# A two-layer diffusion backbone on one core: the first scale blocks multiplied with the weights as stationary operand, in halves

## What is computed

```python
mod_ctx = jax.nn.silu(c_ctx) @ w_mod[l] + b_mod[l]      # mod_lat likewise from c
sh1, sc1, g1, sh2, sc2, g2 = jnp.split(mod, N_MOD, axis=-1)
h = rms_norm(x, p["g_pre_mix"]) * (1.0 + sc1) + sh1
proj = h @ p["w_in"]
```

## Time and profile before

| | us |
|---|---|
| median of 3 runs | 1262.65 (1262.24 to 1262.71) |
| profiled execution | 1259.98 |
| its span, first to last instruction | 1258.2 |
| TensorE busy | 1229.9 (98%) |
| VectorE busy | 847.9 (67%) |
| ScalarE busy | 639.2 (51%) |
| DMA, mean over the span | 157 GB/s read |

### The profile page before, as it was taken

How to read it: one execution, slowest core, us unless ns; L and a number is a source line. 1 busy time by engine, 2 the same in 40 slices (tenths; PEclk the granted TensorE clock), 3 DMA queues, 4 the chain that set the end, 5 groups by cost and what they waited for, 6 DMA issues and landing times.

```text
span 1258.2 us, 19229 instructions
## 1 busy us (share of the span) xinstructions
PE 1229.9 (98%) x7345; PEld 1140.2 (91%) x7345; DVE 847.9 (67%) x1325; ACT 639.2 (51%) x1129; POOL 19.6 (2%) x41
## 2 busy tenths in 40 slices
PE   6999999999989999999999999999999999999998
PEld 4899999988879999998879999998897999999886
DVE  2697594774869879859868895857666748433433
ACT  5478863764454323342255989557546533333322
POOL 0000000200000000000000000021000000000000
PEclk9999999999999999999999999999999999999999
DMA  9645555333347876748815334442234446344451
GB/s 335 221 122 177 189 164 199 108 118 126 114 130 226 265 227 195 236 171 270 287 55 145 108 103 119 132 139 84 69 101 134 139 145 223 121 131 134 160 167 51
DMA packets 131104, 199.34 MB, mean 158 GB/s; under 512 B 10331, under 2 KB 70981, under 8 KB 131013
## 3 DMA queue, kind: packets, MB, share of 16 engines
q1 hardware_dynamic: 131012, 198.11, 49.3%
HBM read 196.16 MB, written 1.92 MB: 157 GB/s over the span
## 4 chain that ended last, share of the span: by engine, by line
PE 88%; DVE 4%; ACT 3%; DMA 2%; issue 1%; SPq 1%; DVEq 0%; ACTq 0%
PE bank L762 19%; PE bank L769 19%; PE bank L770 19%; PE bank L892 5%; PE bank L894 5%; PE bank L893 5%; PE bank L1192 2%; PE bank L1216 1%; ACT sq L1330 1%; PE bank L1201 1%; PE bank L799 1%; DVE weight_low L1691 1%; DMA first_mod<-in_w_mod 1%; PE bank L1038 1%; PE bank L1036 1%
## 5 line engine op out<-in xcount | busy, mean ns | idle before, releaser
L769 PE MATMUL bank<-act_low,weight_high 128*128 128x384 f32 x1440 | 484.7, 337 | 0.3 <-DVE weight_low L1691 0.3
L770 PE MATMUL bank<-act_high,weight_low 128*128 128x384 f32 x1440 | 481.6, 334 | 0.0
L1691 DVE TENSOR_TENSOR weight_low<-raw,weight_high 128x1024 fp32r<-128x1024 f32 (+5 forms) x282 | 320.1, 1151 | 154.1 <-ACT weight_high L1322 153.0
L1322 ACT ACTIVATE weight_high<-raw 128x1024 fp32r<-128x1024 f32 (+5 forms) x282 | 273.4, 996 | 237.4 <-DMA raw<-in_w_ffn_in 79.8
L762 PE MATMUL bank<-act_high,weight_high 128*128 128x384 f32 x1440 | 314.6, 338 | 2.9 <-ACT act_high L1407 1.2
L769 PEld LDWEIGHTS bank<-act_low,weight_high 128*128 128x128 f32 x1440 | 270.3, 188 | 3.9 <-issue 3.2
L770 PEld LDWEIGHTS bank<-act_high,weight_low 128*128 128x128 f32 x1440 | 270.4, 188 | 0.0
L762 PEld LDWEIGHTS bank<-act_high,weight_high 128*128 128x128 f32 x1440 | 252.0, 188 | 11.9 <-issue 5.6
L892 PE MATMUL bank<-weight_high,hid_high 128*128 128x512 f32 x264 | 103.2, 391 | 0.0
L893 PE MATMUL bank<-weight_low,hid_high 128*128 128x512 f32 x264 | 102.8, 389 | 0.0
L894 PE MATMUL bank<-weight_high,hid_low 128*128 128x512 f32 x264 | 102.8, 389 | 0.0
(11 more groups left out here) (265 smaller groups left out, 1443.7 us busy)
## 6 DMA issues: line engine op xcount, KB each, us to landing
raw<-in_w_ffn_in SPq DMA_DIRECT2D x176, 256.0 KB, 4.2
mod_weight<-in_w_mod SPq DMA_DIRECT2D x80, 512.0 KB, 4.7
raw<-in_w_in SPq DMA_DIRECT2D x72, 512.0 KB, 3.8
raw<-in_w_ffn_out SPq DMA_DIRECT2D x44, 512.0 KB, 4.5
first_mod<-in_w_mod SPq DMA_DIRECT2D x4, 2048.0 KB, 13.7
raw<-in_w_o_lru SPq DMA_DIRECT2D x16, 512.0 KB, 3.7
raw<-in_w_out SPq DMA_DIRECT2D x16, 512.0 KB, 3.7
raw<-in_w_o_mla SPq DMA_DIRECT2D x8, 512.0 KB, 4.2
```

The costliest lines, as they stand in the source:

```text
L769: nc.tensor.matmul(o, view[0][:, kk, cols], low[:, k, :], start=False, stop=False)
L770: ins = nc.tensor.matmul(o, view[1][:, kk, cols], high[:, k, :], start=False, stop=k == total - 1)
L1322: nc.scalar.activation(high, w, ACT.Copy).then_inc(*AC.step())
L1691: nc.vector.tensor_tensor(low, w, high.bitcast(F), ALU.subtract).then_inc(*VE.step())
```

## The change

Blocks 2 and 3 (the scales) are each loaded as two DMAs of four chunks (`first_half`), which stand between the first weight loads. Their product is made by `first_columns`: for each of four groups of 128 channels and each contraction chunk, the weight block is the stationary operand and the two columns of `cs` move; the result is already turned, so it has no copy and no fold. The part 0 of a block (chunks 0 to 3) and the part 1 are separate stretches. VectorE then adds bias and makes the gain for group 0 first and for the other three together (`first_scale`). ScalarE makes the high part of chunks 0 and 4 directly from the moved chunk with scale and shift (`high_of`), in two instructions; VectorE still makes `t` of those chunks for the low part. Blocks 0 and 1 stay as they were, with other banks and the fold of block 1 after pair 11. The diff, cut to its core:

```diff
+        def first_column(half, g):
+            if g == 0:
+                return ps[(3, 5)[half]][:, 0:2]
+            return ps[4][:, 8 * half + 2 * g - 2:8 * half + 2 * g]
...
                 if l == 0:
                     first_mods(FIRST[0][:1])
                     vector_rows(0)
-                    first_mods(FIRST[0][1:])
                 for n, load in enumerate(LOADS):
+                    if n == 0 and l == 0:
+                        first_half(FIRST[0][1], 0)
+                    if n == 1 and l == 0:
+                        first_half(FIRST[0][1], 1)
                     if n == 2 and l == 0:
-                        first_mods(FIRST[1])
+                        first_mods(FIRST[1][:1])
+                        first_half(FIRST[1][1], 0)
+                    if n == 3 and l == 0:
+                        first_half(FIRST[1][1], 1)
...
+                def first_columns(half, part):
+                    r = FIRST[half][1]
+                    pe.wait_ge((start_mod, start_mod_late)[part][r], 16)
+                    if part == 0 and half == 0:
+                        pe.wait_ge(*at(AC, "moved", 2))
+                    elif part == 0:
+                        pe.wait_ge(*at(VE, "first", FIRST[1][0]))
+                        pe.wait_ge(*at(VE, "added", FIRST[1][0]))
+                    for g in range(4):
+                        o = first_column(half, g)
+                        for k in range(4 * part, 4 * part + 4):
+                            ins = nc.tensor.matmul(o, first_mod[:, r, k, P * g:P * g + P], cs[:, k, 0:2], start=k == 0 and g < 2,
+                                                   stop=k == C - 1, skip_group_check=True)
+                        if part == 1 and g in (0, 3):
+                            ins.then_inc(*PE.step("columns", r, min(g, 1)))
+
                 def opening_between(i, count):
                     if i == 7:
-                        first_product(1, 0)
+                        first_product(1)
                     if i == 11:
-                        first_fold(1, 0)
-                        first_product(1, 1)
+                        first_fold(1)
                     if i == 13:
-                        first_fold(1, 1)
+                        first_columns(1, 0)
+                    if i == 15:
+                        first_columns(1, 1)
...
                     late_turned(4)
-                    first_product(0, 1)
                     late_turned(5)
-                    first_fold(0, 1)
+                    first_columns(0, 0)
                     late_turned(6)
                     late_turned(7)
+                    first_columns(0, 1)
...
+                    highs("lx0", 0)
+                    for half in range(2):
+                        c = 4 * half
+                        ac.wait_ge(*at(AC, "moved", c))
+                        ac.wait_ge(*at(VE, "scale1", c))
+                        high_of(qkv[:, c, :], scale1, 0, "mix", 0, c, 1)
+                        high_of(qkv[:, c, :], scale1, 0, "mix", 0, c, 0, "hh", "mix", c)
+                        act_highs("mix", 0, "lx0", ({1: 1, 3: 2}, {5: 3})[half], range(c + 1, c + 4))
...
                     def low(c):
+                        ve.wait_ge(*atp(VE, "hfull", pre, c))
                         ve.wait_ge(*atp(AC, "hh", pre, c))
...
+                def first_scale(half, part):
+                    r = FIRST[half][1]
+                    g0, n = (0, 1) if part == 0 else (1, 3)
+                    c0 = 4 * half + g0
+                    ve.wait_ge(*at(PE, "columns", r, part))
+                    bias = par[:, 4 * r + g0:4 * r + g0 + n].rearrange("p (g a) -> p g a", a=1).to_broadcast([P, n, 2])
+                    o = ps[(3, 5)[half]][:, 0:2] if part == 0 else ps[4][:, 8 * half:8 * half + 6]
+                    nc.vector.tensor_tensor(mod[:, 4 * r + g0:4 * r + g0 + n, :], o.rearrange("p (g c) -> p g c", c=2), bias, ALU.add
+                                            ).then_inc(*VE.step(*(("scaled_by", half) if part == 1 else ())))
+                    gain(scale1, 1, "g_pre_mix", ("scale1", c0), slice(c0, c0 + n))
+                    normalise("mix", 0, "fo", "lx0", scale1, 0, {2: 1, 6: 3}, range(c0, c0 + n))
                 if l == 0:
                     for half in range(2):
-                        chunks = slice(4 * half, 4 * half + 4)
-                        first_mods(half)
-                        gain(scale1, 1, "g_pre_mix", ("scale1", half), chunks)
-                        normalise("mix", 0, "fo", "lx0", scale1, 0, ({2: 1}, {6: 3})[half], range(C)[chunks])
+                        first_shift(half)
+                        lows("lx0", 2 * half)
+                        first_scale(half, 0)
+                        first_scale(half, 1)
```

More of the change, by code:

```diff
@@ L375, in program @@
         start_mod = [sem(f"start_mod{r}") for r in NEXT]
+        start_mod_late = {r: sem(f"start_mod_late{r}") for _, r in FIRST}
         start_x = [sem(f"start_x{g}") for g in range(2)]
@@ L484, in first_mods, with first_half @@
                                  ).then_inc(start_mod[r], 16)
+            def first_half(r, half):
+                ks = slice(4 * half, 4 * half + 4)
+                sp.dma_start(first_mod[:, r, ks, :], A["w_mod"][0:1, 512 * half:512 * half + 512, r * 512:r * 512 + 512].rearrange(
+                    "a (k p) n -> p (a k) n", p=P)).then_inc((start_mod, start_mod_late)[half][r], 16)
             def constants_in():
@@ L961, in turn_between, with first_product @@
                     return between
-                def first_product(half, i):
-                    r = FIRST[half][i]
+                def first_product(half):
+                    r = FIRST[half][0]
                     pe.wait_ge(start_mod[r], 16)
                     if half == 1:
-                        pe.wait_ge(*at(AC, "moved", 2 + i))
-                    o = ps[(2, 4)[half] + i]
+                        pe.wait_ge(*at(AC, "moved", 3))
+                    o = ps[(2, 5)[half]]
                     for k in range(C):
@@ L975, in first_product, with first_fold @@
                     ins.then_inc(*PE.step("first", r))
-                def first_fold(half, i):
-                    r = FIRST[half][i]
+                def first_fold(half):
+                    r = FIRST[half][0]
                     pe.wait_ge(start_fold, 16)
                     pe.wait_ge(*at(VE, "first", r))
+                    if half == 1:
+                        pe.wait_ge(*at(VE, "scaled_by", 0))
                     for g in range(4):
-                        ins = nc.tensor.matmul(ps[(1, 4)[half]][:, 8 * i + 2 * g:8 * i + 2 * g + 2],
-                                               tok_flat[:, 512 * r + P * g:512 * r + P * g + P], fold[:, :],
-                                               start=i == 0 and g == 0, stop=True, skip_group_check=True)
+                        ins = nc.tensor.matmul(ps[(1, 4)[half]][:, 2 * g:2 * g + 2], tok_flat[:, 512 * r + P * g:512 * r + P * g + P],
+                                               fold[:, :], start=g == 0, stop=True, skip_group_check=True)
@@ L1000, in _ @@
                         if a == 2:
-                            first_product(0, 0)
+                            first_product(0)
                         pe.wait_ge(start_x[min(a, 1)], 16)
@@ L1007, in _ @@
                     nc.tensor.transpose(ps[0][:, NA:NA + NB], rows_b[0:NB, :], ident[0:NB, 0:NB]).then_inc(*PE.step("par"))
-                    first_fold(0, 0)
+                    first_fold(0)
                     def late_turned(c):
@@ L1400, in seam, with high_of, act_highs @@
                         act_highs(pre, lp, next_job, {1: 2, 4: 3})
-                def act_highs(pre, lp, next_job, after):
+                def high_of(src, dst_scale, shift, pre, lp, c, g, *label):
+                    toks = GROUPS[g][1]
+                    nc.scalar.activation(hh[:, c, toks], src[:, toks], ACT.Identity, scale=dst_scale[:, c, g:g + 1],
+                                         bias=mod[:, shift * C + c, g:g + 1]).then_inc(*AC.step(*label, layer=lp))
+                def act_highs(pre, lp, next_job, after, chunks=range(C)):
                     atp = in_layer(lp)
-                    for c in range(C):
+                    for c in chunks:
                         ac.wait_ge(*atp(VE, "hfull", pre, c))
@@ L1429, in _ @@
                     for c in range(6):
-                        if c == 5:
-                            highs("lx0", 0)
                         ac.wait_ge(*at(PE, "turned", "mix", c))
                         nc.scalar.activation(qkv[:, c, :], turn_bank("fo", c)[:, 0:T], ACT.Copy).then_inc(*AC.step("moved", c))
-                    act_highs("mix", 0, "lx0", {1: 1, 3: 2, 5: 3})
+                    highs("lx0", 0)
[6 more added lines that the diff above has]
+                        act_highs("mix", 0, "lx0", ({1: 1, 3: 2}, {5: 3})[half], range(c + 1, c + 4))
                 ac.wait_ge(*at(VE, "abslam"))
```

(18 more changed lines are left out.)

## The result

The changed kernel took 1273.95 us in the median (1272.73 to 1278.53, 4 executions) beside 1262.45 for the kernel before, a ratio of 1.0105 with a 95% interval from 1.0093 to 1.0117. It is slower by about 11.5 us, not by the 6.3 of the forecast. The profiled execution took 1272.73; its span is 1270.9 against 1258.2, 12.7 us more.

The account below looks back on a forecast made before the run. TensorE's opening was taken to set the end time: +9.0 us net work less 3.45 of closed holes gives +5.6, plus a 0.7 stall, +6.3; from 1262.65 to 1268.9 us, 8 in 10 range 1265.8 to 1275.5.

Parts of the forecast that it names:

- What bounds the kernel: From 43 us on, TensorE sets the end time; a microsecond won or lost in the opening arrives whole.
- the 1.0 us behind weights: A TensorE wait of 1.0 us behind a weight's high part, after 43 us, which could at most absorb opening lateness.
- Removed and added work: TensorE in the opening: 5.39 us of scale products and folds removed, 14.4 us of matmuls added, net +9.0 us.
- the turning point: Price per record of the new matmuls' loads between gain and loss: 0.064 us.
- The holes: Four TensorE waits before lx0's fifth chunk, together 3.45 us, all closing, leaving that chunk +5.6 us later.
- Rival 1: Loads of small matmuls overlap at 0.02 to 0.03 us a record, so the kernel is faster: 1259.6 us; chance 0.06.
- The stall in the seventh chunk: In lx0's second half TensorE waits for VectorE's low part 6: 0.7 us, bounds 0 and 1.3.
- The direct high parts show no gain: At chunks 0 and 4, ScalarE's chain of 1.4 us, or 1.8 the old way, is hidden under 12 matmuls (2.7 us).
- The clock: TensorE's granted clock was expected at 1.00 through the opening; 0.50 anywhere between 20 and 55 us would prove the forecast wrong.
- The likeliest case: Opening +5.6 us plus stall 0.7, giving 1268.9 us, own range 1266.8 to 1271.6; chance 0.57.
- Rival 2: TensorE's clock falls in the opening's two-column stretches, so the kernel is slower still: 1272 to 1278 us; chance 0.31.
- The price of the fall: Rival 2's cost of the lower clock in the opening: +3 to +5 us for one stretch, up to +9 for both.

Follow-up runs that it names:

- the first block alone: Changed kernel with only the first scale block (chunks 0 to 3) made with weights stationary, the second by product and fold: 1270.07 us against 1261.27, ratio 1.0067.

## Why the forecast was wrong

- **What bounds the kernel**: right. A microsecond lost in the opening arrived at the end whole: in the kernel with 128 columns streamed the eighth chunk is 6.4 us late and the span is 7.2 us longer. What was not foreseen is that lateness was not swallowed by the 1.0 us behind weights but added to, by two short waits near 201 us (0.33 and 0.28).
- **Removed and added work**: right. The price of a record is 0.109 us (3.49 over 32) where 0.1125 was taken and the turning point was 0.064. The 0.4 us that this is worth in 128 records is small beside what follows.
- **The holes**: right, all four closed. Rival 1 was out by the price of a record. DMA was never waited for behind the first product.
- **The stall in the seventh chunk**: right at full clock, 0.74 for 0.7. In the changed kernel's profile it is not there; TensorE came to the seventh chunk at 57.60 us instead of 52.32, when VectorE was likely ahead of it.
- **The direct high parts show no gain**: right as far as tested. In the kernel before they gave 0.5 us at the fifth chunk and 0.9994 in time, with 1 inside the interval (0.9984 to 1.0003). In the changed kernel, for which the forecast was made, they were not taken out.
- **The clock**: wrong, and the step that failed. The likeliest case, at 0.57, put the clock's term at nothing: it took the granted clock as 1.00 through the stretches of two streamed columns. No row stood behind that; of the two states in the earlier trace rows the prediction says itself that neither is this case. Rival 2, at 0.31, had the fall, with 1272 to 1278. The two medians were 1273.95 and 1276.08, and the traces have the clock at 0.50 for 13.6 us of the opening in one and for 23.9 in the other. The run with 128 columns streamed shows the difference: +6.5 with the clock at 1.00, +11.5 and +14.5 without. That 1273.95 lies inside the range of 8 in 10, 1265.8 to 1275.5, is owed to the part of rival 2 that the range took in; 1276.08 lies outside.
- **The price of the fall**: rival 2 had up to +9 for both stretches, and the two medians are +5 and +8 over the sum at full clock. For one stretch it had +3 to +5, and that does not hold: the first block alone cost 8.8 us, of which its expectation put 2.0 to work, and the first profile's first stretch cost less than 3. An estimate that comes within 0.8 us of these profiles is half of the time at the lower level: 1.7 and 5.1 us for the two stretches of the changed kernel's first profile, 6.8 and 5.1 for those of its second, 8.5 for the first block alone, whose profiled execution was 10.3 us over that of before. What the forecast did not have is that the fall can come in the first half block and outlast the second.

The Trainium skill, "TensorE: Matmul & The Clock Gate", section Part 1: The HAM clock gate, gives an idle state of 1.2 GHz and a busy one of 2.4 GHz, and warns of a kernel's first matmuls that the moment of the change varies between executions. The traces agree on the levels, 0.50 and 1.00, with 0.21 and 0.109 us a record, and show the moment vary in mid-run too: the first fall came at 29.1 us in one execution and at 23.8 in another.

## What to carry to other kernels

Price a change of operand roles by the loads it makes: a plain f32 matmul with a full stationary block cost two loads, 0.22 us, with 2 columns streamed and with 128, and 32 of them, 7.0 us, were dearer for TensorE than the product and fold that they replaced, 2.7 us. And treat "busy" on TensorE as no promise of its clock: where a change puts stretches of matmuls with very few columns, like the half blocks here, ahead of dense work, forecast the time at the lower level too, and test it by streaming more columns under the same loads. When executions of one kernel differ by some microseconds, look at their granted clocks first.

## What the runs showed of the hardware

- Loads of 128 columns with two columns streamed brought the granted clock from 1.00 to 0.50 while TensorE was listed busy 6.00 of 6.00 us; with 128 columns streamed under the same loads it stayed at 1.00.
- At the lower level a plain f32 load of 128 columns took 0.21 us, not 0.11: loads slow down with the matmuls (6.68 against 3.49 us for 32).
- The same instructions gave different falls: down for 3.4 and 10.2 us from 29.1 and 46.2 in one execution of the changed kernel, for 13.7 and 10.2 from 23.8 and 51.1 in another; 6 us between its fastest and its slowest.
- The kernel before has executions between 1259.7 and 1263.8 us, and they go with their granted clock, 0.999 to 0.996.
- A fall to 0.50 also came in a seam of a kernel without the new matmuls, where TensorE had been idle for half of the time (1.97 of 4 us busy ahead of it in the run of the direct high parts).
